# Eight constant matmuls in each of two TensorE stops at the end of the RWKV preparation

## The reference, cut to what matters

```
def rwkv_prepare(z, p):
    z = token_shift_centred(z, p['rwkv_mu'])
    r, k, v, wl, al, gl = jnp.split(z, RWKV_CUTS, axis=-1)
    ...
    for d in range(2):
        w_log = -softplus(-(w0[d] + tanh(wl) @ w2[d])) - 0.5
        decay = exp(-exp(w_log));  a = sigmoid(a0[d] + al @ a2[d])
        kk = heads(k * k_k[d]);    kk = kk / max(norm(kk), 1e-12)
        kd = heads(k * (1.0 + (a - 1.0) * k_a[d]))
        dirs.append((heads(decay), kd, -kk, kk * heads(a)))

def rwkv_scan(S0, r, w, k, v, a, b, reverse):
    def step(S, inp):
        sa = einsum('bhij,bhj->bhi', S, a_t)
        S = S * w_t + outer(sa, b_t) + outer(v_t, k_t)
        return S, einsum('bhij,bhj->bhi', S, r_t)
    ...
```

## Time and profile before

| | |
|---|---|
| median of three runs | 2457.89 us (2454.81 to 2464.22) |
| the profiled execution's own time | 2458.63 us |
| its span, first to last instruction | 2456.8 us |
| mean granted TensorE clock | 0.952 |
| TensorE busy (matmuls) | 2251.3 us, 92% of the span |
| VectorE, ScalarE, GpSimd busy | 985.5, 674.0, 767.3 us |

### The profile page before, as it was taken

One profiled execution on the slowest core, in us unless ns is written; L12 is line 12 of the kernel. 1 busy time (PEld: TensorE's weight loads), 2 busy tenths in 40 slices (PEclk: granted clock), 3 DMA queues, 4 the chain that ended last, 5 costly groups with the idle time before them and its releaser, 6 DMA issues.

```text
span 2456.8 us, 46004 instructions
## 1 busy us (share of the span) xinstructions
PE 2251.3 (92%) x19396; PEld 1813.2 (74%) x19396; DVE 985.5 (40%) x1477; ACT 674.0 (27%) x1181; POOL 767.3 (31%) x546
## 2 busy tenths in 40 slices
PE   5999889889989799999999899988888988999997
PEld 3888566559968588888888668846658965788886
DVE  3000455565661741414132330055555654532443
ACT  3001255743222310212111220135551222221221
POOL 2332153004123123233232344134203223444443
PEclk8999899978999899999999989899988999999998
DMA  6113000120011212211223223100030013233331
GB/s 253 51 61 117 35 1 0 36 90 3 4 61 48 98 61 62 67 60 60 64 64 128 86 77 101 68 35 1 0 125 3 4 62 120 94 94 94 95 101 60
DMA packets 45404, 162.42 MB, mean 66 GB/s; under 512 B 5504, under 2 KB 5504, under 8 KB 45024
## 3 DMA queue, kind: packets, MB, share of 16 engines
q1 hardware_dynamic: 44480, 157.89, 19.3%
q0 software_dynamic: 800, 2.69, 0.3%
HBM read 158.46 MB, written 2.10 MB: 65 GB/s over the span
## 4 chain that ended last, share of the span: by engine, by line
PE 78%; DVE 13%; ACT 5%; issue 3%; POOL 1%; DMA 1%; SPq 0%; POOLq 0%; ACTq 0%; DVEq 0%
PE ps L1374 74%; PE ps L1649 2%; DVE small L1125 2%; DVE part_h L1022 1%; DVE hT L1015 1%; DVE xT L1040 1%; ACT flat L754 1%; DVE flat L1358 1%; DVE ps L1122 1%; ACT flat L772 1%; DVE flat L1038 1%; DMA flat<-wmod_dram 1%; PE ps L1910 0%; DVE flat L1105 0%; ACT flat L704 0%
## 5 line engine op out<-in xcount | busy, mean ns | idle before, releaser
L1374 PE MATMUL ps<-part_hi,wparts 128*128 128x512 f32 (+1 forms) x3072 | 815.1, 353 | 27.2 <-DVE part_h L1022 8.6
L1374 PEld LDWEIGHTS ps<-part_hi,wparts 128*128 128x128 f32 x3072 | 545.0, 191 | 116.3 <-DVE part_h L1022 14.0
L508 POOL TENSOR_TENSOR wparts<-flat,wparts 128x1024 fp32r<-128x1024 f32 x184 | 447.5, 2432 | 535.2 <-ACT wparts L938 529.5
L1374 PE MATMUL ps<-flat 64*64 64x32 f32 (+8 forms) x8812 | 491.5, 264 | 54.4 <-ACT flat L772 28.3
L1374 PEld LDWEIGHTS ps<-flat 64*64 64x64 f32 (+4 forms) x8812 | 381.3, 147 | 150.2 <-issue 72.3
L1374 PE MATMUL ps<-part_h,wparts 128*128 128x512 f32 (+1 forms) x1344 | 474.2, 353 | 0.0
L1374 PE MATMUL ps<-part_mlp,wparts 128*128 128x512 f32 (+1 forms) x1536 | 417.1, 358 | 15.2 <-DVE part_h L1022 10.2
L1374 PE MATMUL ps<-part_lo,wparts 128*128 128x512 f32 x960 | 341.3, 356 | 0.0
L1374 PEld LDWEIGHTS ps<-part_mlp,wparts 128*128 128x128 f32 x1536 | 275.1, 191 | 62.5 <-DVE part_h L1022 12.3
L938 ACT ACTIVATE wparts<-flat 128x1024 fp32r<-128x1024 f32 x112 | 118.8, 1061 | 704.2 <-PE ps L1374 704.2
L1374 PEld LDWEIGHTS ps<-part_h,wparts 128*128 128x128 f32 x1344 | 257.8, 192 | 32.2 <-issue 0.2
(11 more groups left out here) (201 smaller groups left out, 1978.3 us busy)
## 6 DMA issues: line engine op xcount, KB each, us to landing
flat<-w_dram SPq DMA_DIRECT2D x128, 512.0 KB, 3.6
flat<-wmod_dram SPq DMA_DIRECT2D x88, 512.0 KB, 5.2
flat<-win_dram SPq DMA_DIRECT2D x40, 512.0 KB, 3.6
flat<-wout_dram SPq DMA_DIRECT2D x16, 512.0 KB, 3.8
hT<-wmod_dram SPq DMA_DIRECT2D x8, 512.0 KB, 7.2
xT<-xT_dram SPq DMA_DIRECT2D x8, 384.0 KB, 6.3
flat<-rope_dram SPq DMA_DIRECT2D x2, 1024.0 KB, 5.7
out_dram<-xT SPq DMA_DIRECT2D x8, 256.0 KB, 2.0
```

What stands on the lines that cost most here:

```text
L508: pool.tensor_tensor(wlo[q % 2], src, whi[q % 2], ALU.subtract).then_inc(s_used[q], 1)
L1374: return pe.matmul(out, lhsT, rhs, start=start, stop=stop)
```

## The change

Two calls are added on TensorE, one behind each `mod_columns` at the end of the RWKV preparation. Each runs eight matmuls of 128 x 512 on the constant `kf` into PSUM columns 3584 to 4095. Nothing waits for them, and they wait for nothing. They run in both layers: 32 matmuls in all, 64 records.

```diff
                 ring_row(5)
                 pe.wait_ge(s_modrow, MOD_FROM[l] + 5)
                 mod_columns(scan_rows, 3, COL_SCAN)
+                keep_clock(3584, 8)
                 ring_row(4)
                 pe.wait_ge(s_modrow, MOD_FROM[l] + 6)
                 mod_columns(scan_rows, 1, COL_SCAN + 24)
+                keep_clock(3584, 8)
 
                 pe.wait_ge(s_prep, 5 * l + 5)
```

## The result

The changed kernel takes 2472.9 us (median of 7 runs, 2462.0 to 2481.0) against 2457.9. The ratio is 1.0061, with a 95% interval of 1.0046 to 1.0076: 11 to 19 us slower. The forecast was 2462 with a range of 2454 to 2472, so it had the sign of its sum right, but a quarter of the size (3.8 us of 15.0), and it gave "slower by over 0.5%" only 0.12.

A forecast was written before the change was run, and what follows sets the result against it. TensorE, 92% busy, was taken to bound the kernel, so added matmuls cost their length beyond its idle stops. First layer +3.5 us and second +0.3 gave +3.8 on 2458.63, 2462.4, about 2462 for the median; range 2454 to 2472.

The forecast's parts named there:

- the fills: TensorE behind each `mod_columns`: 7.0 us a fill at full clock, 9.9 us for the first layer's first, starting at half clock.
- the start of the scan: Scan starts 5.3 us later in the first layer, 1.8 in the second; its 128 records gain 1.8 and 1.5 us.
- ends before it does now: Second layer, ahead of VectorE's L1230: `ring_row` (1843.4 against 1842.4) does not hold VectorE, which arrives at about 1846.
- the bound of −2.0 us: Largest gain at the first layer's scan start: half of the 4.1 us spent at half clock, 549.29 to 553.4.
- it costs nothing: First layer: GpSimd's L587 starts 0.9 us later, ends at 555.3, before TensorE finishes `keyed` at about 558.
- what else waits: First layer: VectorE's L1230 waits for `ring_row`, moving its chain 0.9 us, covered by the second fill; GpSimd's L587 checked too.
- the later low stretch: Half-clock stretch of about 17 us after the bonus, both layers: zero change, bounded at −2 to +3 us.
- a sign of being wrong: After the bonus: the prediction is wrong if the low stretch changes by several microseconds in both layers.
- Rival 2: Every fill meets a low clock; three fills take 9.9 instead of 7.0 us, sum +12.5, about 2470.5; chance 0.14.
- Rival 3: The 17 us low stretch in the scan goes as well in both layers: −13, 2445; chance 0.06.

The follow-up runs named there:

- fills of 8 + 8: Eight constant matmuls behind each of the two `mod_columns` calls, against the kernel before; the changed kernel itself, 2472.9 us, ratio 1.0061.
- The late scan: Kernel before, no fills; TensorE, idle, also waits ahead of the scan until GpSimd has done both halves of L587; 2489.5 us, ratio 1.0125.
- the gates: GpSimd's bonus products held back until VectorE has done L1257 and L1259 for both halves; on the changed kernel 2468.0 us, on the second fill only 2464.2 us.
- 4 + 6: First fill cut to four matmuls and second to six, bonus unchanged; 2462.0 us, ratio 1.0008 to the kernel before.
- The gated kernel with six constant matmuls at the bonus: Changed kernel, GpSimd held back until VectorE's first transposes, two constant matmuls each ahead of, amid and behind the bonus; 2457.4 us, 1.0003 to the kernel before.
- Six matmuls at the bonus: Two constant matmuls each ahead of, amid and behind the twelve bonus matmuls, against the kernel before: 0.9981 without fills, 0.9967 with fills of four and six.

## Why the prediction was wrong

**Right: the fills and the start of the scan.** A fill of 16 records was priced at 9.9 us where it meets a low clock and 7.0 elsewhere; they took 9.18, 7.11, 7.11 and 7.11 in the changed kernel's profile. (The forecast's 7.0 for the second layer's first fill was luck in part: in the four other profiles with fills of 8 + 8 it took 9.1 to 9.3.) The scan's start was put at +5.3 and +1.8 us and came at +4.9 and +1.6. Its 128 records were put at 3.6 to 3.7 us and took 3.72. VectorE did wait for `ring_row`, 0.63 us at L1230, and the fill covered it. Two slips in the working did no harm. For the second layer it says that `ring_row` "ends before it does now" beside 1843.4 against 1842.4, which is later; VectorE arrives at about 1846 either way. And it takes the first layer's changes of level 0.5 us too late, so that the bound of −2.0 us would have been −1.8.

**Wrong: "it costs nothing" for GpSimd.** The step that failed first is the sentence on what else waits. It asked whether GpSimd would be late for TensorE and found that it would be early. It did not ask what GpSimd's being early would put beside VectorE. `s_prep` releases GpSimd, while TensorE, busy with the fill, holds VectorE back; GpSimd's L611 and L617 move forward onto the two L1257, which went from 0.68 and 0.84 us to 2.01 and 1.82. That is 2.3 us on the chain, and the price of the idle that it makes is larger: the clock fell among the 64x32 matmuls for 10.2 us, which costs 5.1. From the scan's start to the bonus, −1.8 + 2.3 + 5.1 = +5.6 against +5.4 measured. The late scan shows that the shift slows L1257 without a fill, and the gates show that the stretch goes with it. The gate is worth 4.9 us on the medians of the changed kernel (ratio 1.0061 to 1.0030), and 10.5 where only the second fill runs (1.0060 to 1.0017).

The Trainium skill, page "SBUF — State Buffer", section "Who interferes with whom", says that a VectorE operation with both inputs in SBUF contends with a GpSimd operation that reads SBUF, and that the contention is an exclusive lock. L1257 has both operands in SBUF, and the trace agrees: both times it ends 0.56 us after the GpSimd product that it met, and the next product of the pair is 0.4 to 0.5 us longer. L1254, with one operand in PSUM, stayed at 1.22 to 1.23 us.

**Wrong: zero for the later low stretch.** It was bounded at −2 to +3 us over both layers, from the two layers of one trace that agreed on 17.1 us. In the profiles of kernels with fills and an unchanged bonus it was 20.5 or 23.9 us, except with the second fill alone and no gate, where it stayed at 17.1. In the changed kernel's profile it was 20.5 in both layers, 3.4 us more at half clock, by an estimate 1.7 us a layer; the forecast had named a change of several microseconds in both layers as a sign of being wrong. With 4 + 6, where nothing else was wrong, it took back all that the full clock at the scan's start had won. The agreement of the two layers was not a measure of how far it can move: both had the same code ahead of them.

**The sum.** In the profiles the first layer, from the first columns to the fill after the scan, is +4.9 (start), +5.4 (to the bonus) and −0.2 (the rest); the second is +1.6, −0.1 and +1.7. Together +13.2; the rest of the program was 2.1 us shorter, which makes the 11.1 us of the span. The forecast had +7.1 of late starts less 3.3 of gains. The failing terms are the +5.4, where it had −1.8, and the later stretch, whose cost is the second layer's +1.7. In the first layer waits hid it: between the bonus and the third step TensorE stood idle 3.5 us where it had been 6.0. The gated kernel with six constant matmuls at the bonus takes both away, and the 17.1 us stretch of before with them, and is level with before.

**The rivals.** Rival 2 named about the right time, 2470.5, by the wrong mechanism: in the changed kernel's profile no fill but the first met a low clock. In the four other profiles with fills of 8 + 8 the second layer's first fill did too, never a second fill, so a part of it may stand in some runs. Rival 3 held that the later stretch might vanish; it does not by itself. Its price, half of the stretch, is borne out roughly. Six matmuls at the bonus are an estimated 5.3 us a layer; by the medians, each against its own before, they gained 3.9 us without fills, where 17.1 less 10.6 would be 6.5, and 9.8 us with 4 + 6, where 23.8 less 10.6 would be 13.2. The advice of the Trainium skill, page "TensorE: Matmul & The Clock Gate", section "Why this matters for your kernels", against long idle gaps held up only in part, as the forecast had said: with 4 + 6 the scan started at full clock, and the clock fell behind it while TensorE was busy.

**Still open.** What sets off the clock's fall after the bonus, why it comes sooner (1.3 and 1.2 us after the bonus begins with 4 + 6, 4.2 and 3.9 before), and why runs of one kernel differ by up to 29 us. The change of level depends on what ran ahead, in a way that these traces do not resolve. No trace was taken of the changed kernel's 2480 us runs; that they have the stretch ahead of the bonus in both layers, as the profile of the second fill alone has, or a slow first fill in both, is only argued. No run left the bonus out, and the gate and the bonus matmuls were not tried in one kernel with fills of 4 + 6.

## What to carry to other kernels

A filler for an engine's wait must end before the wait does. If it outlasts it, everything that the same event releases on other engines runs ahead of this one, and the question is then not only who is late but who now runs side by side. Size a fill to the stop (here 4 and 6 instead of 8 and 8) and then look for the next place where the clock falls, since a fill that only moves the fall wins nothing. A stretch at half clock in which the engine is fully busy is the larger prize: here six dense matmuls around twelve 2-column ones gave 0.9981 without any fill, and fills of 4 + 6 alone 1.0008.

## What the runs showed of the hardware

Being busy did not keep the clock up. Matmuls 32 columns wide on a quarter of the array ran at 1.2 GHz for 17.1 us before the change and for 20.5 us in the changed kernel, TensorE 100% busy, until the clock rose while they were still running. The same matmuls, reached at 2.4 GHz with nothing between them, went on at 2.4 GHz for 28.1 us. The falls ahead of the bonus came 0.2 to 2.2 us after waits of 0.78 to 1.10 us, and those behind it 1.2 to 4.2 us after the beginning of the 2.8 us of 2-column matmuls; waits of 0.42 to 0.47 us were not followed by one. A VectorE operation of 0.68 us with both inputs in SBUF took 1.8 to 2.3 us when it met a GpSimd product of 1.8 to 2.1 us.
